# Ending every block of a 39-block kernel with the semaphore-only barrier

## The chip, the cores and the metric

One Trainium2 chip, one of its cores. The metric is the device time of one execution in microseconds (us); three runs of the kernel before give a median of 3190.18 us.

## The reference

Three transformer blocks run one after the other on an input of 512 tokens and 1024 features, all in float32. In short:

```python
x = layer_norm(a*x + 0.5*swiglu_ffn(x))                  # block 1: FFN 1024 -> 2816 -> 1024
x = layer_norm(a*x + parallel_mixers(x))                 # gated delta rule, 31-tap convolution, gates
x = layer_norm(a*x + memory_cross_attention(x, mem))     # 4 heads over 256 memory rows
x = layer_norm(a*x + 0.5*swiglu_ffn(x))
x = x + [retention(x), nsa(x)] @ w_out                   # block 2: retention beside compressed,
                                                         #   selected and window attention
x = ...neighbourhood attention and MLA, gated, then FFN  # block 3
```

Most of the arithmetic is in the products with 202 weight tiles of 128 x 2048 numbers.

## The kernel before

Activations lie feature-major in SBUF (`arena`, 56 units of 128 x 512). Each float32 weight tile is loaded by SyncE (line 185, `stream_load`), split into a high part by ScalarE (line 198, `split_hi`) and a low part by GpSimd (line 207, `stream_split_lo`), two buffers each; TensorE then makes three products a tile part (lines 228 to 230, `three_products`). The loads and splits run one or two tiles ahead of TensorE, through all the phases: the split of the first tile of a phase is made at the end of the phase before it.

The program is a row of phases, and each phase is one `nc.Block()`: a region in which every engine has its own list of instructions, and at whose end all five engines meet. There are 18 places in the source that open a block, and the program runs 39 of them: `phase_stream` (line 549) 14 times, `phase_ffn_in` (342), `phase_ffn_out` (396) and `phase_attention_pairs` (1667) three times each, `phase_head_norm` (882) and `phase_rope` (1891) twice, and one each of `phase_start` (277), the delta rule's phases (970, 1082, 1155, 1239), `phase_attention` (1482), `phase_mla_norms` (1849), `phase_norm_2` (1939), `phase_compress` (2061), `phase_retention` (2167), `phase_mla_in` (2267) and the last one in `program` (2408). The line of a block is also the line under which the profile files its barrier.

The barrier at the end of a block is not in the source; the trace shows its instructions. Every engine's sequencer issues a DRAIN. The DRAINs of TensorE, VectorE, ScalarE and SyncE each raise one counting semaphore; GpSimd's DRAIN raises none. GpSimd's sequencer then waits in an EVENT_SEMAPHORE for four arrivals, and raises a second semaphore in another EVENT_SEMAPHORE; the four others wait for that one in an EVENT_SEMAPHORE each. So GpSimd is the hub. A further barrier of this form, at line 2594, stands ahead of the first block and is made by the constructor of the program, not by a block.

GpSimd issues no DMA in this kernel: SyncE and ScalarE issue all of them. Nothing else orders work between blocks that a semaphore doesn't; apart from the splits that run ahead, the first instruction of a phase starts when the barrier lets it. A phase that ends with a layer norm (line 396, and part of those of 549) ends with ScalarE's reciprocal square root (line 490); the next phase starts with VectorE scaling by it (line 534) and ScalarE's affine step (line 526).

Of the kernel before, what the change touches and what calls it, by code (L numbers as in the profile page):

```python
# [273 lines left out]
def phase_start(K):  # L274

    nc, dram = K.nc, K.dram
    with nc.Block() as block:
        @block.sync
        def _(sp):
            sp.dma_start(K.raw[:, 0, :, :], dram["stream"][0]).then_inc(K.s("raw_loaded_0").sem, 16)  # L280
            for i in range(2):
                sp.dma_start(K.A[:, 4 * i:4 * i + 4, :], dram["x_t"][:, 4 * i:4 * i + 4, :]).then_inc(K.s(f"x_in_{i}").sem, 16)
            sp.dma_start(K.raw[:, 1, :, :], dram["stream"][1]).then_inc(K.s("raw_loaded_1").sem, 16)
            sp.dma_start(K.vecs[:, :], dram["vecs"]).then_inc(K.s("loaded").sem, 16)
            sp.dma_start(K.mats[:, :, :], dram["mats"]).then_inc(K.s("loaded").sem, 16)
            sp.dma_start(K.small[:, 0:320], dram["small"]).then_inc(K.s("loaded").sem, 16)

        @block.scalar
        def _(act):
            split_hi(K, act, 0, 1, 0, 1)  # L290
            nc.scalar.nop().then_inc(K.s("bank_free_0").sem, K.s("bank_free_0").n(2))

        @block.vector
        def _(dve):
            nc.vector.nop().then_inc(K.s("bank_free_1").sem, K.s("bank_free_1").n(2))
    K.end_block()
# [39 lines left out]
def phase_ffn_in(K, name, weight=0.5, norm=None):  # L336


    nc = K.nc
    silu, h_ready, hhi_ready = K.s("silu_ready"), K.s("h_ready"), K.s("h_hi_ready")  # L340
    sg, h = K.A[:, 52:54, :], K.A[:, 54:56, :]
    with nc.Block() as block:  # L342
        @block.sync
        def _(sp):
            stream_load(K, sp, name)
            if isinstance(norm, FirstSplit):
                sp.wait_ge(K.s("loaded").sem, 48)

        @block.gpsimd
        def _(pool):  # L350
            if norm:
                norm.pool(pool)
            stream_split_lo(K, pool, name)

        @block.tensor
        def _(pe):
            stream_pe(K, pe, name, split=norm is not None)

        @block.scalar
        def _(act):  # L360
            if norm:
                norm.act(act)

            def evac(t, g, slot, times):
                wait_bank(K, act, g, 0)
                nc.scalar.activation(sg[:, slot, :], K.ps[:, 2 * slot, :], ACT.Silu).then_inc(silu.sem, silu.n(1, times))  # L366
            stream_act(K, act, name, evac)

        @block.vector
        def _(dve):  # L370
            if norm:
                norm.dve(dve)

            def evac(t, g, slot, times):
                wait_bank(K, dve, g, 1)
                dve.wait_ge(silu.sem, silu.at(t + 1))
                nc.vector.scalar_tensor_tensor(h[:, slot, :], sg[:, slot, :], weight, K.ps[:, 2 * slot + 1, :],  # L377
                                               ALU.mult, ALU.mult).then_inc(h_ready.sem, h_ready.n(1, times))
                dve.wait_ge(h_ready.sem, h_ready.at(t + 1))
                nc.vector.nop().then_inc(K.s("bank_free_0").sem, K.s("bank_free_0").n(1, times))  # L380
                nc.vector.nop().then_inc(K.s("bank_free_1").sem, K.s("bank_free_1").n(1, times))
                at = bass.ds(t, 1) if not isinstance(t, int) else slice(t, t + 1)
                nc.vector.tensor_copy(K.hhi[:, at, :], h[:, slot:slot + 1, :]).then_inc(hhi_ready.sem, hhi_ready.n(1, times))
                dve.wait_ge(hhi_ready.sem, hhi_ready.at(t + 1))
                nc.vector.tensor_tensor(K.hlo[:, at, :], h[:, slot:slot + 1, :], K.hhi[:, at, :].bitcast(F32),
                                        ALU.subtract)
            stream_dve(K, dve, name, evac)
    K.end_block()


def phase_ffn_out(K, name):

    nc, s = K.nc, K.s
    norm = LayerNorm(K, 0, lambda eng, c: eng.wait_ge(s("sum_taken").sem, s("sum_taken").at(c + 1)),
                     K.pair[:, 8:12, :], mean_bank=0, var_bank=1)
    with nc.Block() as block:
        @block.sync
        def _(sp):
            stream_load(K, sp, name)

        @block.gpsimd
        def _(pool):
            stream_split_lo(K, pool, name)
            norm.stats_pool(pool)

        @block.scalar
        def _(act):
            stream_act(K, act, name)
            norm.stats_act(act)

        @block.tensor
        def _(pe):
            def body(t, g, uses, slot, times):
                pe.wait_ge(K.s("lo_ready").sem, g + 1)
                for j in range(2):
                    f = bass.ds(2 * t + j, 1) if not isinstance(t, int) else slice(2 * t + j, 2 * t + j + 1)
                    for m in range(KC):
                        last = three_products(K, K.ps[:, m:m + 1, :], K.whi[:, slot, 8 * j + m, :],
                                              K.wlo[:, slot, 8 * j + m, :], K.hhi[:, f, :], K.hlo[:, f, :],
                                              isinstance(t, int) and t == 0 and j == 0,  # L420
                                              isinstance(t, int) and t == TILES[name] - 1 and j == 1)
                        if isinstance(t, int) and t == TILES[name] - 1 and j == 1 and m < KC - 1:
                            last.then_inc(s("sum_ready").sem, s("sum_ready").n())
                    last.then_inc(K.s(("first_done", "tile_done")[j]).sem, 1)
            n, first = TILES[name], FIRST_TILE[name]
            body(0, first, 0, first % 2, 1)
            loops = (n - 3) // 2
            with pe.Fori(0, loops) as i:
                for j in range(2):
                    body(2 * i + (1 + j), 2 * i + (first + 1 + j), 0, (first + 1 + j) % 2, loops)  # L430
            for t in range(1 + 2 * loops, n):
                body(t, first + t, 0, (first + t) % 2, 1)
            norm.stats_pe(pe)

        @block.vector
        def _(dve):
            for m in range(KC):
                if m < KC - 1:
                    dve.wait_ge(s("sum_ready").sem, s("sum_ready").at(m + 1))
                else:  # L440
                    wait_bank(K, dve, FIRST_TILE[name] + TILES[name] - 1, 1)
                nc.vector.scalar_tensor_tensor(K.A[:, m, :], K.A[:, m, :], ALPHA, K.ps[:, m, :], ALU.mult,  # L442
                                               ALU.add).then_inc(s("sum_taken").sem, s("sum_taken").n())
            norm.stats_dve(dve)
# [98 lines left out]
def phase_stream(K, label, names, pe=None, act=None, dve=None, load=None, load_next=None, pe_last=None, presplit=None, width=T,  # L543
# [2 lines left out]

    with K.nc.Block() as block:
        @block.sync  # L550
        def _(sp):
            if load:
# [320 lines left out]
def phase_head_norm(K, label, items, scratch, eps=RMS_EPS, after=None, store=False, source=None):  # L873


    nc, s = K.nc, K.s
# [2 lines left out]

    def taken(i):  # L880
        return source[:, i, :] if source is not None else K.A[:, items[i][0], :]
    with nc.Block() as block:
        @block.scalar
        def _(act):
            def square(i):
# [75 lines left out]
def phase_gdn_matrices(K):  # L961

    nc, s = K.nc, K.s
# [3 lines left out]
        return W[:, 2 * kind + h % 2, :]  # L967
    LEVEL, DEC, EXPG, MD = range(4)
    TILES_AT = [slice(P * i, P * i + P) for i in range(NT)]
    with nc.Block() as block:  # L970
        @block.gpsimd
        def _(pool):
            for h in range(GDN_HEADS):
# [101 lines left out]
def phase_gdn_inverse(K):  # L1075

    nc, s = K.nc, K.s
# [1 line left out]
    items = [(level, h) for level in (2, 4, 8, 16, 32) for h in range(GDN_HEADS)]  # L1079
    n = len(items)  # L1080
    turns = n - GDN_HEADS
    with nc.Block() as block:
        @block.gpsimd
        def _(pool):
            for x, (level, h) in enumerate(items):
# [65 lines left out]
def phase_gdn_tokens(K):  # L1151

    nc, s = K.nc, K.s
    A, W = K.A, K.pair
    with nc.Block() as block:
        @block.tensor
        def _(pe):
            def turn(h):
# [49 lines left out]
def phase_gdn_scan(K):  # L1208
# [27 lines left out]
        return ap.rearrange("p (k s n) -> p k s n", k=2, s=2)  # L1236
    finish = [0, 2, 4, 6, 1, 3, 5, 7]
    TURNED = [0, 1, 4, 5, 6, 7]
    with nc.Block() as blk:
        @blk.vector  # L1240
        def _(dve):
            nc.vector.memset(W[:, 4:6, :], 0.0).then_inc(s("scan_zero").sem, s("scan_zero").n())
# [209 lines left out]
def phase_attention(K, label, heads, p_unit, pt_unit, load=None):  # L1452
# [26 lines left out]
    def col(at, x):  # L1479
        return K.small[:, at + x % 4:at + x % 4 + 1]  # L1480

    with nc.Block() as block:
        @block.sync
        def _(sp):
            if load:
# [141 lines left out]
def phase_attention_pairs(K, label, pairs, p_unit, pt_unit, load=None):  # L1627
# [36 lines left out]
    def cols(at, x):  # L1664
        return K.small[:, at + 2 * (x % 4):at + 2 * (x % 4) + 2]

    with nc.Block() as block:
        @block.sync
        def _(sp):
            if load:  # L1670
# [174 lines left out]
def phase_mla_norms(K):  # L1845

    nc, s = K.nc, K.s
    sq = K.pair
    with nc.Block() as block:
        @block.sync  # L1850
        def _(sp):
            sp.dma_start(sq[:, 8:13, :], K.dram["mla_w"]).then_inc(s("reloaded").sem, s("reloaded").n(16))
# [30 lines left out]
def phase_rope(K, label, chunks, matrix, cos, sin, load=None, rows=P, copies=None):  # L1883
# [4 lines left out]

    def wait_added(eng, x):
        eng.wait_ge(s("rope_added").sem, s("rope_added").at(x + 1))  # L1890
    with nc.Block() as block:  # L1891
        @block.sync
        def _(sp):
            if load:
# [41 lines left out]
def phase_norm_2(K):  # L1936

    nc, s = K.nc, K.s
    with nc.Block() as block:
        @block.vector  # L1940
        def _(dve):
            Affine(K, 0, "ln4_g", "ln4_b", split=False).dve(dve)
# [98 lines left out]
def phase_compress(K):  # L2041
# [16 lines left out]
    def hid(kind, m, g):  # L2058
        at = HID + 128 * kind + 64 * m + 32 * g
        return K.small[:, at:at + N_CMP]  # L2060
    with nc.Block() as block:
        @block.sync
        def _(sp):
            for i in range(1, 4):
# [88 lines left out]
def phase_retention(K):  # L2153
# [10 lines left out]

    def weighted(x, side):
        return W[:, 2 * (x % 3) + side, :]
    with nc.Block() as block:
        @block.tensor
        def _(pe):
            def scores(x):  # L2170
# [90 lines left out]
def phase_mla_in(K):  # L2261
# [2 lines left out]
    A, W = K.A, K.pair  # L2264
    uq = W[:, 8:11, :].rearrange("p a b -> p (a b)").rearrange("p (k n) -> p k n", k=2)
    ukv = W[:, 11:13, :].rearrange("p a b -> p (a b)")
    with nc.Block() as block:
        @block.sync
        def _(sp):
            sp.dma_start(A[:, 52:54, :], K.dram["rope_3"]).then_inc(s("reloaded").sem, s("reloaded").n(16))  # L2270
# [125 lines left out]
def program(nc, dram):  # L2396
# [8 lines left out]
    block2(K)  # L2405
    block3(K)
    last = Affine(K, 0, "ln2_g_3", "ln2_b_3", split=False)
    with nc.Block() as block:  # L2408
        @block.vector
        def _(dve):  # L2410
            last.dve(dve)
# [194 lines left out]
```

## Time and profile before

| what | value |
|---|---|
| runs, median (lowest to highest) | 3190.18 us (3188.05 to 3190.51) |
| the profiled execution | 3194.44 us, its span 3192.7 us |
| TensorE busy | 2924.4 us, 92% of the span |
| TensorE weight loads | 2282.5 us, 71%, beside the products |
| VectorE, ScalarE, GpSimd busy | 32%, 32%, 36% |
| mean granted TensorE clock | 0.95 of full speed |
| blocks (barriers) | 39, and one barrier ahead of them |

The profile is one execution on the chip. PE is TensorE, PEld its weight loads, DVE VectorE, ACT ScalarE, POOL GpSimd, SP SyncE; a q behind the name (POOLq) is the engine's sequencer, which waits, branches and issues. DRAIN and EVENT_SEMAPHORE are sequencer instructions and don't count as busy. A DRAIN is recorded from where the sequencer reaches it to where the engine's issued work is done, so a long one is mostly the engine's own last operations.

### The profile page before, as it was taken

To read this page: it belongs to the slowest core of one execution; us is meant where nothing else is said; L and a number is where in the kernel's file an instruction comes from. 1 tells how busy PE (TensorE), PEld (TensorE's weight loads), DVE (VectorE), ACT (ScalarE), POOL (GpSimd) and SP (SyncE) were. 2 spreads that over 40 slices of the span, in tenths; PEclk is the share of its full clock that TensorE was granted. 3 is DMA by queue.
4 is the path that set the end of the run, shared out by engine and by line. 5 is a ranking of instruction groups with operands and counts; after the bars stand their busy time and mean duration, and the time that the engine had idled before them with its cause. 6 is when DMAs were issued, how large, how long until landed. Compare 5 with 4: busy or idle time off the path is not lost. (4 is left out here: it accounts for less than half of the span.)

```text
span 3192.7 us, 35648 instructions
## 1 busy us (share of the span) xinstructions
PE 2924.4 (92%) x14270; PEld 2282.5 (71%) x14270; DVE 1034.9 (32%) x1727; ACT 1019.8 (32%) x1439; POOL 1162.7 (36%) x379
## 2 busy tenths in 40 slices
PE   8999999999989988889999899877899789999998
PEld 6887788886688767668878587344787436678876
DVE  2110216997334431431110300555300635431101
ACT  3331222234444223233321322244122444143312
POOL 4443443444363346144444442100344011444442
PEclk9999999999999999999999899877999889999999
DMA  4222231243100233122222124000223001122221
GB/s 153 104 92 92 79 119 66 100 144 125 67 1 28 106 119 119 40 79 92 92 95 103 42 103 160 33 3 1 83 102 125 1 24 40 66 92 92 98 87 66
DMA packets 40847, 258.01 MB, mean 81 GB/s; under 512 B 4128, under 2 KB 5536, under 8 KB 13088
## 3 DMA queue, kind: packets, MB, share of 16 engines
q1 hardware_dynamic: 37136, 248.09, 21.9%
q10 hardware_dynamic: 3600, 8.39, 0.7%
q8 instruction: 76, 1.25, 0.2%
q14 instruction: 35, 0.29, 0.0%
HBM read 243.88 MB, written 12.58 MB: 80 GB/s over the span
## 5 line engine op out<-in xcount | busy, mean ns | idle before, releaser
L207 POOL TENSOR_TENSOR weights_lo<-weights_raw,weights_hi 128x2048 fp32r<-128x2048 f32 x201 | 940.8, 4681 | 1567.5 <-ACT weights_hi L198 1567.5
L228 PE MATMUL psum<-x_hi,weights_hi 128*128 128x512 f32 (+1 forms) x2560 | 1009.3, 394 | 100.3 <-DVE x_lo L331 54.5
L229 PE MATMUL psum<-x_lo,weights_hi 128*128 128x512 f32 (+1 forms) x2560 | 1003.0, 392 | 0.0
L230 PE MATMUL psum<-x_hi,weights_lo 128*128 128x512 f32 (+1 forms) x2560 | 1002.2, 391 | 0.0
L198 ACT ACTIVATE weights_hi<-weights_raw 128x2048 fp32r<-128x2048 f32 x202 | 386.6, 1914 | 833.3 <-PE psum L230 725.8
L228 PEld LDWEIGHTS psum<-x_hi,weights_hi 128*128 128x128 f32 x2560 | 489.3, 191 | 217.8 <-issue 84.9
L230 PEld LDWEIGHTS psum<-x_hi,weights_lo 128*128 128x128 f32 x2560 | 489.1, 191 | 100.9
L229 PEld LDWEIGHTS psum<-x_lo,weights_hi 128*128 128x128 f32 x2560 | 489.8, 191 | 98.9
L377 DVE SCALAR_TENSOR_TENSOR arena<-arena,psum 128x512 f32<-128x512 f32 x66 | 45.4, 688 | 554.8 <-PE psum L230 554.8
L228 PE MATMUL psum<-h_hi,weights_hi 128*128 (+1 forms) x528 | 207.7, 393 | 7.7 <-PEq L342 7.7
L229 PE MATMUL psum<-h_lo,weights_hi 128*128 (+1 forms) x528 | 207.2, 392 | 0.0
L230 PE MATMUL psum<-h_hi,weights_lo 128*128 (+1 forms) x528 | 206.9, 392 | 0.0
L715 DVE SCALAR_TENSOR_TENSOR psum<-arena,vecs,psum 128x511 f32<-128x511 f32 (+17 forms) x240 | 159.5, 735 | 10.4 <-ACT arena L674 7.8
L442 DVE SCALAR_TENSOR_TENSOR arena<-arena,psum 128x512 f32<-128x512 f32 x24 | 16.3, 687 | 351.0 <-PE psum L230 351.0
L228 PEld LDWEIGHTS psum<-h_hi,weights_hi 128*128 128x128 f32 x528 | 100.2, 190 | 29.8 <-issue 8.8
L230 PEld LDWEIGHTS psum<-h_hi,weights_lo 128*128 128x128 f32 x528 | 100.2, 190 | 21.0
L229 PEld LDWEIGHTS psum<-h_lo,weights_hi 128*128 128x128 f32 x528 | 100.2, 190 | 20.8
L366 ACT ACTIVATE arena<-psum 128x512 f32<-128x512 f32 x66 | 39.5, 598 | 201.1 <-PE psum L230 201.1
L511 POOL TENSOR_TENSOR x_lo<-arena,x_hi 128x512 fp32r<-128x512 f32 x48 | 63.0, 1321 | 98.1 <-DVE x_hi L504 98.1
L1725 DVE TENSOR_TENSOR psum<-psum,arena 128x256 f32<-128x256 f32 (+2 forms) x64 | 36.9, 577 | 188.9 <-PE psum L1681 186.3
L1681 PE MATMUL psum<-arena 64*128 64x512 f32 (+4 forms) x256 | 92.4, 688 | 3.8 <-PEq L1891 2.7
L1911 POOL TENSOR_TENSOR pair_scratch<-arena 96x512 f32<-96x512 f32 (+1 forms) x17 | 21.4, 1265 | 187.8 <-DVEq L1918 179.7
(258 smaller groups left out, 3068.1 us busy)
## 6 DMA issues: line engine op xcount, KB each, us to landing
weights_raw<-in_stream SPq DMA_DIRECT2D x202, 1024.0 KB, 4.8
keep_gates<-arena ACTq DMA_DIRECT2D x24, 256.0 KB, 2.0
arena<-keep_gates SPq DMA_DIRECT2D x3, 2048.0 KB, 9.6
arena<-in_na_bias SPq DMA_DIRECT2D x1, 3584.0 KB, 12.9
arena<-in_x_t SPq DMA_DIRECT2D x2, 1024.0 KB, 8.0
keep_x<-arena ACTq DMA_DIRECT2D x1, 2048.0 KB, 8.5
keep_yc<-arena SPq DMA_DIRECT2D x1, 2048.0 KB, 7.0
arena<-keep_yc SPq DMA_DIRECT2D x1, 2048.0 KB, 14.0
```

The source lines that it names most:

```text
L198: K.nc.scalar.activation(K.whi[:, slot, :, :], K.raw[:, slot, :, :], ACT.Copy).then_inc(K.s("hi_ready").sem, 1)
L207: K.nc.gpsimd.tensor_tensor(K.wlo[:, 1 - slot, :, :], K.raw[:, 1 - slot, :, :], K.whi[:, 1 - slot, :, :].bitcast(F32), ALU.subtract).then_ ...
L228: K.nc.tensor.matmul(out, whi, xhi, start=start, stop=False)
L229: K.nc.tensor.matmul(out, whi, xlo, start=False, stop=False)
L230: return K.nc.tensor.matmul(out, wlo, xhi, start=False, stop=stop)
L366: nc.scalar.activation(sg[:, slot, :], K.ps[:, 2 * slot, :], ACT.Silu).then_inc(silu.sem, silu.n(1, times))
L377: nc.vector.scalar_tensor_tensor(h[:, slot, :], sg[:, slot, :], weight, K.ps[:, 2 * slot + 1, :], ALU.mult, ALU.mult).then_inc(h_ready.sem ...
L511: K.nc.gpsimd.tensor_tensor(K.xlo[:, c, :], K.A[:, first_unit + c, :], K.xhi[:, c, :].bitcast(F32), ALU.subtract).then_inc(K.s("x_split"). ...
L715: ins = nc.vector.scalar_tensor_tensor(acc[:, back:], K.A[:, 8 + c, :T - back], w, acc[:, back:], ALU.mult, ALU.add)
L1681: last = nc.tensor.matmul(K.ps[:, scores_bank(x) + side, :w], q, k[:, :w], start=True, stop=True)
L1725: nc.vector.tensor_tensor(out, out, bias, ALU.add).then_inc(s("att_bias").sem, s("att_bias").n())
L1911: nc.gpsimd.tensor_tensor(W[:rows, 12 + x % 2, :], A[:rows, c, :], cos, ALU.mult).then_inc(s("rope_cos").sem, s("rope_cos").n())
```

## The change

All 18 places open their block with an argument:

```diff
@@ phase_start @@
-    with nc.Block() as block:
+    with nc.Block(no_gpsimd_drain=True) as block:
@@ phase_stream @@
-    with K.nc.Block() as block:
+    with K.nc.Block(no_gpsimd_drain=True) as block:
@@ phase_gdn_scan @@
-    with nc.Block() as blk:
+    with nc.Block(no_gpsimd_drain=True) as blk:
```

and in the same way at the other fifteen. The description of the argument says that the engines other than GpSimd are then retired with a plain drain, and that the engines meet in a barrier made of semaphore instructions alone, with no drain on GpSimd. No other line changes.

## Rows read from the trace of the kernel before

**Rows 1.** The page, part 1: busy time, share and instructions of each engine.

```profile
PE 2924.4 (92%) x14270; PEld 2282.5 (71%) x14270; DVE 1034.9 (32%) x1727; ACT 1019.8 (32%) x1439; POOL 1162.7 (36%) x379
```

**Rows 2.** The page, part 3: every DMA queue of the core, packets, MB.

```profile
q1 hardware_dynamic: 37136, 248.09, 21.9%
q10 hardware_dynamic: 3600, 8.39, 0.7%
q8 instruction: 76, 1.25, 0.2%
q14 instruction: 35, 0.29, 0.0%
```

**Rows 3.** Line 396, 380 to 394 us: op xcount, ns min/median/max, first and last start.

```profile
L396 POOLq EVENT_SEMAPHORE  x2: 17/17/17, 392.9 to 393.0; - x2
L396 POOLq DRAIN  x1: 1356/1356/1356, 381.0 to 381.0; - x1
...
L396 PEldq DRAIN  x1: 3000/3000/3000, 389.2 to 389.2; - x1
L396 ACTq DRAIN  x1: 679/679/679, 392.2 to 392.2; - x1
L396 SPq EVENT_SEMAPHORE  x1: 17/17/17, 393.0 to 393.0; - x1
...
L396 DVEq EVENT_SEMAPHORE  x1: 21/21/21, 393.0 to 393.0; - x1
L396 PEldq EVENT_SEMAPHORE  x1: 51/51/51, 393.0 to 393.0; - x1
```

**Rows 4.** Timeline, 391 to 394.7 us: start, us, engine, line, idle before.

```profile
392.19 0.66 ACT L490 ACTIVATE psum<-psum,vecs 128x512 f32<-128x512 f32 x1 [1.74 <-PE psum L479]
393.14 1.88 DVE L534 TENSOR_TENSOR arena<-arena,psum 128x512 f32<-128x512 f32 x3 [4.66 <-PEq L396]
...
393.87 1.52 ACT L526 ACTIVATE arena<-arena,vecs 128x512 f32<-128x512 f32 x2 [1.02 <-DVE arena L534]
```

**Rows 5.** Line 549 over the whole span: the barriers of all 14 streaming blocks.

```profile
L549 POOLq EVENT_SEMAPHORE  x28: 17/17/17, 497.6 to 2796.9; - x28
...
L549 POOLq DRAIN  x14: 1351/4708/7249, 480.5 to 2784.9; - x14
L549 ACTq DRAIN  x14: 259/679/1931, 488.9 to 2796.1; - x14
```

**Rows 6.** Line 549, 1232 to 1239 us: one barrier.

```profile
L549 POOLq DRAIN  x1: 4711/4711/4711, 1233.2 to 1233.2; - x1
...
L549 ACTq DRAIN  x1: 414/414/414, 1237.5 to 1237.5; - x1
```

**Rows 7.** Timeline, 1236.5 to 1242 us, around that barrier.

```profile
1233.22 4.61 POOL L207 TENSOR_TENSOR weights_lo<-weights_raw,weights_hi 128x2048 fp32r<-128x2048 f32 x1 [1.81 <-ACT weights_hi L198]
...
1237.51 0.38 ACT L1823 ACTIVATE arena<-psum 128x256 f32<-128x256 f32 x1 [2.49 <-PE psum L1444]
...
1238.20 1.88 DVE L534 TENSOR_TENSOR arena<-arena,psum 128x512 f32<-128x512 f32 x3 [50.57 <-PEq L549]
```

**Rows 8.** Line 1667, 2075 to 2237 us: the barrier of an attention block.

```profile
L1667 POOLq DRAIN  x1: 34/34/34, 2075.1 to 2075.1; - x1
...
L1667 DVEq DRAIN  x1: 730/730/730, 2235.2 to 2235.2; - x1
```

**Rows 9.** Line 2408, the last block's barrier.

```profile
L2408 POOLq DRAIN  x1: 41/41/41, 3183.7 to 3183.7; - x1
...
L2408 SPq DRAIN  x1: 7/7/7, 3192.4 to 3192.4; - x1
```

**Rows 10.** Who waited for whom, whole span: us in total, times, longest.

```profile
DVE arena L534 <- PEq L396: 14.0, 3, 4.7
...
POOL weights_lo L308 <- POOLq L277: 7.5, 1, 7.5
```

More of the change, by code:

```diff
@@ L341, in phase_ffn_in @@
     sg, h = K.A[:, 52:54, :], K.A[:, 54:56, :]
-    with nc.Block() as block:
+    with nc.Block(no_gpsimd_drain=True) as block:
         @block.sync
@@ L395, in phase_ffn_out @@
                      K.pair[:, 8:12, :], mean_bank=0, var_bank=1)
-    with nc.Block() as block:
+    with nc.Block(no_gpsimd_drain=True) as block:
         @block.sync
@@ L881, in taken @@
         return source[:, i, :] if source is not None else K.A[:, items[i][0], :]
-    with nc.Block() as block:
+    with nc.Block(no_gpsimd_drain=True) as block:
         @block.scalar
@@ L969, in phase_gdn_matrices @@
     TILES_AT = [slice(P * i, P * i + P) for i in range(NT)]
-    with nc.Block() as block:
+    with nc.Block(no_gpsimd_drain=True) as block:
         @block.gpsimd
@@ L1081, in phase_gdn_inverse @@
     turns = n - GDN_HEADS
-    with nc.Block() as block:
+    with nc.Block(no_gpsimd_drain=True) as block:
         @block.gpsimd
@@ L1154, in phase_gdn_tokens @@
     A, W = K.A, K.pair
-    with nc.Block() as block:
+    with nc.Block(no_gpsimd_drain=True) as block:
         @block.tensor
@@ L1480, in col @@
         return K.small[:, at + x % 4:at + x % 4 + 1]
-    with nc.Block() as block:
+    with nc.Block(no_gpsimd_drain=True) as block:
         @block.sync
@@ L1665, in cols @@
         return K.small[:, at + 2 * (x % 4):at + 2 * (x % 4) + 2]
-    with nc.Block() as block:
+    with nc.Block(no_gpsimd_drain=True) as block:
         @block.sync
@@ L1848, in phase_mla_norms @@
     sq = K.pair
-    with nc.Block() as block:
+    with nc.Block(no_gpsimd_drain=True) as block:
         @block.sync
@@ L1890, in wait_added @@
         eng.wait_ge(s("rope_added").sem, s("rope_added").at(x + 1))
-    with nc.Block() as block:
+    with nc.Block(no_gpsimd_drain=True) as block:
         @block.sync
@@ L1938, in phase_norm_2 @@
     nc, s = K.nc, K.s
-    with nc.Block() as block:
+    with nc.Block(no_gpsimd_drain=True) as block:
         @block.vector
@@ L2060, in hid @@
         return K.small[:, at:at + N_CMP]
-    with nc.Block() as block:
+    with nc.Block(no_gpsimd_drain=True) as block:
         @block.sync
@@ L2166, in weighted @@
         return W[:, 2 * (x % 3) + side, :]
-    with nc.Block() as block:
+    with nc.Block(no_gpsimd_drain=True) as block:
         @block.tensor
@@ L2266, in phase_mla_in @@
     ukv = W[:, 11:13, :].rearrange("p a b -> p (a b)")
-    with nc.Block() as block:
+    with nc.Block(no_gpsimd_drain=True) as block:
         @block.sync
@@ L2407, in program @@
     last = Affine(K, 0, "ln2_g_3", "ln2_b_3", split=False)
-    with nc.Block() as block:
+    with nc.Block(no_gpsimd_drain=True) as block:
         @block.vector
```

## The prediction

> **What bounds the kernel now.** I read the busy times first. TensorE is busy for 92% of the span [rows 1], and the three other compute engines for about a third each, so most of the time is products that no barrier touches; a change to the barriers can only act in the seams between the 39 blocks. The chain that ended last reaches back only through the last 9 us of the span and says nothing of the other seams, so I went on to the barrier's own instructions, block by block, under the line of each block. Rows 3 are one such barrier, the one that ends the first FFN's output phase. The reader is to see three things there. Each engine has a DRAIN that starts where its sequencer runs out of instructions and lasts until its issued work is done. The sequencer of GpSimd reaches its DRAIN at 381.0 us and has done with it at 382.4 us (1356 ns). The last to arrive is ScalarE, whose DRAIN starts at 392.2 and lasts 679 ns, to 392.9. So GpSimd stands ready 10.5 us before the barrier can open, and its DRAIN is not what anybody waits for. Then come two semaphore instructions of GpSimd, at 392.9 and 393.0, and one of each other engine.
>
> What the whole barrier costs is seen beside it [rows 4]: ScalarE's last operation ends at 392.19 + 0.66 = 392.85 us, VectorE's first of the next phase starts at 393.14. The seam is 0.29 us, and everything that a different barrier could win or lose is a change to these 0.29 us, times 39.
>
> **What is removed.** GpSimd's DRAIN, 39 times. It could be dear in two ways, and both are read off.
>
> First, it could have DMAs to wait for. The queue table has two queues of the hardware's dynamic kind and two of instructions, and none that GpSimd feeds [rows 2]; where GpSimd has nothing of its own in flight its DRAIN takes 34 to 41 ns [rows 8, 9]. The long ones, 1351 to 7249 ns in the 14 streaming blocks [rows 5], are GpSimd's own last subtraction or addition: in rows 6 and 7 the DRAIN of 4711 ns starts with the split of 4.61 us and ends with it.
>
> Second, GpSimd could be the last to arrive. I went through the 39 barriers in this way and compared where each DRAIN ends. ScalarE, VectorE, TensorE or SyncE is last in all of them. The closest is the one at 1238 us [rows 6]: GpSimd's DRAIN ends at 1233.2 + 4.7 = 1237.9, ScalarE's at 1237.5 + 0.4 = 1237.9, a tie. Its seam [rows 7] goes from 1237.51 + 0.38 = 1237.89 to 1238.20, 0.31 us, so the tie costs at most 0.02 us over the 0.29 of rows 4. The typical one has GpSimd ahead by 5 to 12 us, and the widest by 160 us (rows 8: 2075.1 against 2235.2 + 0.7). So what hides the removed DRAIN is the tail of the other engines, the layer norm of rows 3 or the last evacuations, and the removal is worth 39 times nothing, with 0.02 us at the tie. The stall that would be dropped isn't one; next late is who was late before.
>
> One wait in the list of waits looks like GpSimd's barrier and isn't: POOLq L277 is charged with 7.5 us [rows 10]. That is the first block, where everybody waits for the first weight tile; the charge goes to the releasing engine, as the 14.0 us on PEq L396 do, and neither falls with a DRAIN.
>
> **What is added.** The four other engines keep a DRAIN, but a plain one. In the kernel before their arrival is an update that the DRAIN itself makes, as there is no arrival instruction of theirs in rows 3: one EVENT_SEMAPHORE each, which is the wait for the release. With a plain DRAIN and a barrier of semaphore instructions alone, the arrival must be an instruction of its own behind the DRAIN, one more on each of four queues. Only that of the engine that arrives last lies on the path. Nothing is queued behind it on that engine but the release wait, and for that one everyone waits, so its price is paid in full in each seam; after the barrier the first instruction of the next phase starts later by the same amount, and nothing hides that, since the next phase has no instruction before it.
>
> Its price has bounds in the rows. From below it is the duration alone: 17 ns on ScalarE or SyncE, 21 on VectorE, 51 on TensorE [rows 3]. From above it is the pitch of GpSimd's two consecutive semaphore instructions, 392.9 to 393.0, 0.1 us. Between them lies the mean step of the seam: 0.29 us hold four handoffs (last operation to GpSimd's wait, wait to raise, raise to the release waits, these to the next operation), 0.07 us each. I take 0.08 us, since a step of that mean size with rounding is nearest and this step also carries its own 17 to 21 ns. Bounds: 39 x 0.017 = 0.7 us and 39 x 0.1 = 3.9 us; sum: 39 x 0.08 = 3.1 us. The hub's two instructions and the four release waits I cost at nothing, as they are there before.
>
> **The sum.** The profiled execution took 3194.44 us (span 3192.7 us) and would take 3194.44 + 3.1 = 3197.5 us. The median of the runs lies 4.3 us below the profiled execution, so the forecast for the median is 3190.18 + 3.1 = 3193.3 us, +0.1%. A measurement of this kernel can tell about 0.2% (6.4 us) from no change, so this counts as no change.
>
> **The rivals.**
>
> *A longer relay (slower).* The argument's barrier need not have one hub. If the engines hand the arrival along in a row and the release back, five engines make eight hops instead of the four handoffs of today. At the 0.07 us of a handoff that is 0.56 instead of 0.29 us; the seam grows by 0.27, times 39 is 10.5 us: 3200.7 us, slower. It decides for slower from 0.165 us more for each seam (6.4 / 39). For it speaks that a semaphore-only form is said to be another barrier than the one with drains; against it, that the hub scheme in rows 3 is already made of EVENT_SEMAPHORE instructions once the DRAINs are over, and could be kept. The Trainium skill, page Runtime: NRT & Kernel Launch, section on the preamble and postamble, describes such a serpentine over five engines for the runtime's own barrier, at 355 ns (44 ns a hop, eight hops). No row here has that form; against the 0.29 us of the seam in rows 4 it would add some 0.07 us by that figure, an estimate from that page, 2.5 us in all, and the case would fall inside no change.
>
> *The arrival costs nothing.* The arrival may still be made by the plain DRAIN, or the extra instruction may overlap the DRAIN's end. Then nothing on the path changes and the time is 3190.2 us. This is also the case in which the change does nothing but drop 39 hidden DRAINs. For it speaks rows 3, where the sequencers of four engines stand at their DRAIN long before it ends.
>
> *A direct exchange (a little faster).* If all engines raise and wait for one count, GpSimd's two instructions leave the path and one arrival comes in: four handoffs become three, -0.07 x 39 = -2.7 us, 3187.5 us. Even a barrier that cost nothing would give only 39 x 0.29 = 11.3 us, so faster by 6.4 us needs more than half of the seam to go.
>
> *GpSimd runs past the barrier.* Without its DRAIN GpSimd's last subtraction may go on into the next block. Nobody gains, as shown, but the port or the next wait could be met otherwise; in the seam of rows 7 that is under 0.1 us once, and I give it no time.
>
> **How the numbers follow.** The separate arrival 0.50 (3193.3, by its bounds 3190.9 to 3194.1); arrival at no cost 0.22 (3190.2); relay 0.17 (3200.7); direct exchange 0.08 (3187.5); something not seen 0.03, half of it faster. The runs before differ by 2.5 us, which goes on both ends. The range must leave out at most 0.2: it takes in the direct exchange down to 3186.0 and above reaches to 3200.0, so that the lower part of the relay (a seam longer by 0.08 to 0.25 us) is in it and its upper part out. Faster by over 0.2% (below 3183.8) has 0.02; slower by over 0.2% (above 3196.6) has the relay with most of its 0.17 and a share of the unseen, 0.16; the rest, 0.82, is within 0.2%.
>
> **What would show each step right or wrong.** In the profile after, no DRAIN of GpSimd under a block's line (one stays at 2594, ahead of the blocks); two EVENT_SEMAPHORE instead of one for each other engine in each of 39 barriers, so some 156 instructions more and 39 fewer; the seam of rows 4 at 0.37 instead of 0.29 us, and ScalarE still last there. The relay would show in EVENT_SEMAPHORE starts that follow one another over the engines and a seam of 0.5 us or more. A direct exchange would show GpSimd with the same pair as everybody. The prediction would be wrong if GpSimd's DRAIN did something that its record doesn't show, if seams changed by more than 0.165 us, or if time moved away from the seams, say in TensorE's products [rows 1], where the change has no business.

## The result and the profile after

| | runs | median, us | lowest to highest |
|---|---|---|---|
| before | 6 | 3188.98 | 3185.42 to 3190.51 |
| changed | 6 | 3198.72 | 3192.68 to 3203.67 |

The ratio is 1.0026, interval 1.0014 to 1.0038: slower by 8.3 us of the kernel before, 4.5 to 12.1. (The two medians of the table lie 9.7 us apart; the text goes by the ratio on record.) The forecast was 3193.3 us with a range of 3186.0 to 3200.0. Measured again in two later sessions, the ratio was 1.0012 (0.9999 to 1.0025) and 1.0015 (1.0006 to 1.0024), where the forecast stood at 1.0010. So the changed kernel is slower by 0.1 to 0.3%, about what one measurement can tell from nothing; over all runs together it is 4.9 us with an error of 0.9.

The profiled execution of the changed kernel took 3192.68 us, less than that of the kernel before (3194.44). Its page:

```profile
span 3190.9 us, 35765 instructions
...
PE 2918.2 (91%) x14270; PEld 2279.8 (71%) x14270; DVE 1029.6 (32%) x1727; ACT 1019.5 (32%) x1439; POOL 1163.1 (36%) x379
```

TensorE's busy time is 6.2 us lower than in rows 1, with the same number of instructions. A single execution of either kernel can come out ahead: the mean granted clock of this one was 0.957, that of the kernel before 0.954, and how time goes with this clock is read further down.

The barrier that answers to rows 3, in the changed kernel (line 396, 377 to 394 us; engine, instruction, count, ns min/median/max, first and last start):

```profile
L396 DVEq EVENT_SEMAPHORE  x2: 21/21/21, 385.8 to 390.3; - x2
L396 PEldq EVENT_SEMAPHORE  x2: 51/51/51, 389.4 to 390.3; - x2
L396 ACTq EVENT_SEMAPHORE  x2: 17/17/17, 390.1 to 390.3; - x2
L396 POOLq EVENT_SEMAPHORE  x2: 17/17/17, 390.1 to 390.2; - x2
L396 DVEq DRAIN  x1: 4897/4897/4897, 380.8 to 380.8; - x1
L396 PEldq DRAIN  x1: 3002/3002/3002, 386.4 to 386.4; - x1
L396 ACTq DRAIN  x1: 679/679/679, 389.4 to 389.4; - x1
L396 SPq EVENT_SEMAPHORE  x1: 17/17/17, 390.3 to 390.3; - x1
```

There is no DRAIN of GpSimd any more. ScalarE, VectorE and TensorE have two EVENT_SEMAPHORE each where rows 3 had one: the first is the arrival, a separate instruction behind the DRAIN (ScalarE: DRAIN 389.4 + 0.679, arrival at 390.1), the second the wait for the release. SyncE's first lies outside this window. GpSimd has its two, as before, and is still the hub. ScalarE still arrives last. In the whole program there are 117 instructions more, 156 arrivals less 39 DRAINs (35765 against 35648).

The seam that answers to rows 4, in the timeline (start, duration, engine, line):

```profile
389.37 0.66 ACT L490 ACTIVATE psum<-psum,vecs 128x512 f32<-128x512 f32 x1 [1.74 <-PE psum L479]
390.38 1.28 DVE L534 TENSOR_TENSOR arena<-arena,psum 128x512 f32<-128x512 f32 x2 [4.72 <-PEq L396]
```

From the end of ScalarE's operation, 389.37 + 0.66 = 390.03 us, to the start of VectorE's it is 0.35 us, against 0.29.

And the one that answers to rows 7, where GpSimd and ScalarE were level:

```profile
1229.62 4.61 POOL L207 TENSOR_TENSOR weights_lo<-weights_raw,weights_hi 128x2048 fp32r<-128x2048 f32 x1 [1.81 <-ACT weights_hi L198]
...
1233.92 0.38 ACT L1823 ACTIVATE arena<-psum 128x256 f32<-128x256 f32 x1 [2.49 <-PE psum L1444]
...
1234.67 0.69 DVE L534 TENSOR_TENSOR arena<-arena,psum 128x512 f32<-128x512 f32 x1 [52.20 <-PEq L549]
```

From 1233.92 + 0.38 = 1234.30 to 1234.67 it is 0.37 us, against 0.31. GpSimd's split ends at 1234.23 and isn't waited for; nothing came of that, since ScalarE ends at 1234.30.

Compared seam by seam, from the end of the last DRAIN to the first operation behind the barrier, the 38 seams between blocks are longer by 0.049 to 0.112 us, the median by 0.062. The trace gives three sizes: mostly 0.053 us where ScalarE arrives last (0.049 to 0.060), about 0.07 where VectorE does (0.060 to 0.077), and 0.112 at the one seam where TensorE does. The sum is 2.5 us.

### The profile page after: what moved, and what is told of

Read it like the earlier page. It is cut to its first block and busy times, and to the rows that moved or that the text cites. A ratio compares the mean times of both kernels' runs of the same rounds, so it can differ in the third digit from the quotient of the medians.

```text
span 3190.9 us, 35765 instructions
## 1 busy us (share of the span) xinstructions
PE 2918.2 (91%) x14270; PEld 2279.8 (71%) x14270; DVE 1029.6 (32%) x1727; ACT 1019.5 (32%) x1439; POOL 1163.1 (36%) x379
## 6 DMA issues: line engine op xcount, KB each, us to landing
arena<-in_na_bias SPq DMA_DIRECT2D x1, 3584.0 KB, 12.9
arena<-keep_yc SPq DMA_DIRECT2D x1, 2048.0 KB, 13.8
```

## The experiments

**The kernel before against itself, and how far a ratio can be trusted.** No line is changed.

> The kernel before, unchanged, against itself. Every theory: ratio 1.000. It tells how far two medians of one program lie apart on this chip, which is what the other ratios of this call are to be read against. If it comes out at 1.001 or more either way, half or more of the measured 1.0026 of the change can be spread of the runs.

Measured: 0.9989 (0.9979 to 0.9998), with 12 runs against 35. In a later session:

> The kernel before against itself, again: 1.000, clock 0.956. Its distance from 1 is the error of such a ratio.

Measured: 0.9995 (0.9986 to 1.0004). A third run of the same program came about unmeant. The kernel before was to have bare nops in its seams:

```diff
@@ Kernel.end_block @@
             s.base += s.pending
             s.pending = 0
+        nc = self.nc
+        for _ in range(8):
+            for eng in (nc.sync, nc.tensor, nc.vector, nc.scalar, nc.gpsimd):
+                eng.nop()
```

> The kernel before, with eight sequencer nops on each engine behind each of the 38 blocks but the last. A nop of a sequencer takes about what an arrival instruction takes, so each seam grows by eight times that, 0.4 to 0.7 us, 15 to 27 us in all, if time of a seam is paid once: ratio 1.005 to 1.0085. Theory of amplification (a seam's delay moves TensorE's half-speed stretches and costs three times what the seam shows): 45 us or more, 1.014.

Measured: 0.9995 (0.9985 to 1.0005). The trace has 35648 instructions, as many as the kernel before: a nop that neither waits nor raises is not in the program that ran, so it says nothing of seams and is one more control. The seams of its trace sum to 10.2 us, against 10.1 in the kernel before, so the expected 15 to 27 us failed with the edit. The three miss 1 by 0.0011, 0.0005 and 0.0005, all downwards, and the interval of the first (up to 0.9998) leaves out 1, though the program is the same: the intervals are somewhat too narrow. The first also meets the condition of its expectation (0.001 or more either way), so a large part of the 1.0026 of the first measurement can be spread of the runs, and it needed repeating. A ratio of 1.0008, what the seams alone would give, can't be told from 1.

**The changed kernel again.**

> The changed kernel again. Arrival theory (each seam is longer by one semaphore instruction, some 0.05 to 0.12 us, 39 times, about 2.5 us, and nothing else): ratio 1.0008, and the ratio of 1.0026 falls back. Theory of a cost outside the seams (a further 6 us): 1.0026 again, and the blocks themselves longer in the trace.

Measured: 1.0012 (0.9999 to 1.0025).

> The changed kernel a third time. Its seams are longer by 2.5 us in all in its traces. If that is all that it costs beside the spread of half-speed stretches: ratio 1.0008 plus or minus 0.0012, and mean granted clock somewhere in the range of the control's. If the change also lowers the clock for good, as in the two measurements so far (0.954 against 0.956): 1.002 and clock 0.954 again.

Measured: 1.0015 (1.0006 to 1.0024), mean granted clock of its runs 0.9543, beside 0.9557 for the kernel before in the same session and 0.9554 for its control (in the earlier session 0.9541 beside 0.9559 and 0.9569). The seams of its profiled execution are longer by 2.4 us in all. The ratio lies between the two expected, within the 0.0012 allowed to the seams alone; the clock is the lower one.

**The DRAIN put back.** The arrival stays separate and only GpSimd's DRAIN returns, as its last instruction in each block.

```diff
+@contextlib.contextmanager
+def block_with(nc):
+    with nc.Block(no_gpsimd_drain=True) as block:
+        yield block
+
+        @block.gpsimd
+        def _(pool):
+            pool.drain()
...
-    with nc.Block(no_gpsimd_drain=True) as block:
+    with block_with(nc) as block:
```

> The changed kernel, with a DRAIN put back as the last instruction of GpSimd in each of the 39 blocks, so that only the separate arrival of the other four is left of the change. Arrival theory: as the changed kernel, seams longer by 0.05 to 0.12 us, ratio 1.0008. Theory that the missing DRAIN costs the further 6 us (GpSimd running on into the next block): the 6 us come back, and the ratio is below that of the changed kernel in this call by 0.002.

Measured: 1.0022 (1.0009 to 1.0034); 1.0012 for the changed kernel in the same session.

> The changed kernel with GpSimd's DRAIN put back, again. Its seams are as long as those of the changed kernel (2.4 against 2.5 us in all). If the DRAIN is worth nothing: equal to the changed kernel of this call within 0.0012. If the 3 us that it was slower last time are the DRAIN's: 0.001 above the changed kernel again.

Measured: 1.0019 (1.0007 to 1.0030), beside 1.0015. Its GpSimd DRAINs, all 39 under one line (columns as in rows 3):

```profile
L109 POOLq DRAIN  x39: 34/1357/7254, 0.7 to 3190.0; - x39
```

They are as short and as long as in rows 5 and 8, and the seam of the first FFN is that of the changed kernel, 389.95 + 0.66 = 390.61 to 390.96, 0.35 us:

```profile
389.95 0.66 ACT L503 ACTIVATE psum<-psum,vecs 128x512 f32<-128x512 f32 x1 [1.74 <-PE psum L492]
390.96 1.28 DVE L547 TENSOR_TENSOR arena<-arena,psum 128x512 f32<-128x512 f32 x2 [4.72 <-PEq L104]
```

So the DRAIN can be there or not; the seam's length comes from the arrivals alone. The theory that GpSimd running on costs the further 6 us falls: it asked for a ratio 0.002 below that of the changed kernel, and with the DRAIN back nothing is won. Whether the DRAIN itself costs something can't be told: the two ratios are higher by 0.0010 and 0.0004, inside their intervals, and its seams sum to 2.4 us like the others.

**The same delay by another instruction.** The kernel before with its own barriers; behind each of 38 blocks every engine raises a counting semaphore of its own once, or four times.

```diff
@@ Kernel.end_block @@
             s.pending = 0
+        for eng, name in ((self.nc.sync, "sp"), (self.nc.tensor, "pe"), (self.nc.vector, "dve"), (self.nc.scalar, "act"),
+                          (self.nc.gpsimd, "pool")):
+            for _ in range(1):        # 4 in the second kernel
+                eng.nop().then_inc(self.s("count_" + name).sem, 1)
```

> The kernel before, with its own barriers, and behind each of 38 blocks one nop that raises a counting semaphore on each of the five engines. That is the same kind of delay as the separate arrival (some 0.07 us in a seam, 2.7 us in all) by another instruction in another place. Seams alone: ratio 1.0008 against the kernel before, mean granted clock as before (0.956). Theory that a longer seam also costs TensorE clock: clock 0.954 as in the changed kernel, and 1.002 as there. Theory that the changed kernel's lower clock has to do with its barrier's form: clock 0.956 here.

> The same with four of them on each engine in each of 38 seams, about 0.28 us a seam, 10.6 us in all. Seams alone: ratio 1.0033. If each us of seam costs three through the clock: 30 us, 1.010. If the extra of the changed kernel is a chance of where its half-speed stretches fall, not a thing that grows with the seams: 1.0033 plus or minus 0.001, whatever the clock.

Measured: 1.0018 (1.0009 to 1.0027) with one, 1.0044 (1.0030 to 1.0059) with four. The seam behind the first FFN with one:

```profile
392.06 0.66 ACT L494 ACTIVATE psum<-psum,vecs 128x512 f32<-128x512 f32 x1 [1.74 <-PE psum L483]
393.11 1.88 DVE L538 TENSOR_TENSOR arena<-arena,psum 128x512 f32<-128x512 f32 x3 [4.75 <-PEq L400]
```

392.72 to 393.11, 0.39 us, 0.10 more than in rows 4. With four:

```profile
393.08 0.66 ACT L494 ACTIVATE psum<-psum,vecs 128x512 f32<-128x512 f32 x1 [1.74 <-PE psum L483]
394.41 1.88 DVE L538 TENSOR_TENSOR arena<-arena,psum 128x512 f32<-128x512 f32 x3 [5.03 <-PEq L400]
```

393.74 to 394.41, 0.67 us, 0.38 more. Over the 38 seams the traces sum to 3.8 and 13.8 us. Measured are 5.7 us (2.9 to 8.6) and 14 us (10 to 19). The second seam is longer than the 0.28 us expected, and its ratio lies just above the 1.0033 plus 0.001. The clock of the first came out at 0.9546, that of the second at 0.9553, beside 0.9549 (standard error 0.0004) for the kernel before in the same session: neither is clearly lower.

**A whole barrier more.** `self.nc.all_engine_barrier()` in the same place of the kernel before.

> The kernel before with a second all-engine barrier, with drains, behind each of 38 blocks. It measures a whole barrier with nothing to wait for: the seam of 0.27 to 0.29 us less the first instruction's issue, some 0.2 us, 38 times: 7.6 to 11 us, ratio 1.0024 to 1.0034. Amplification by three would be 1.008 or more.

Measured: 1.0044 (1.0029 to 1.0058), 14 us (9 to 19), with a clock of 0.9535 (0.0006); more than the 7.6 to 11 us expected. The seam:

```profile
390.15 0.66 ACT L491 ACTIVATE psum<-psum,vecs 128x512 f32<-128x512 f32 x1 [1.74 <-PE psum L480]
391.44 1.28 DVE L535 TENSOR_TENSOR arena<-arena,psum 128x512 f32<-128x512 f32 x2 [5.00 <-PEq L149]
```

390.81 to 391.44, 0.63 us, 0.34 more than in rows 4; times 38 that is 12.9 us, and over all 38 seams the trace sums to 14.5 us more. The added DRAINs of GpSimd, which has nothing to do there:

```profile
L149 POOLq DRAIN  x38: 34/41/108, 7.7 to 3195.5; - x38
```

From the two larger ones: a us of seam costs about a us, 14 measured against 13.8 and 14 against 14.5 in the traces, whether by one instruction or by a barrier. The amplification by three (each us of seam costing three through the clock) is excluded, as it would be 1.008 to 1.010 for these two. The smaller delays cost about 2 us more than their seams (5.7 against 3.8 here, 4.9 against 2.5 in the changed kernel over all its runs), the larger ones don't; that is inside the error for the one raise, and no run here explains it.

**Where the DRAIN does matter.** GpSimd gets DMAs of its own: at the end of each block four copies of 1 MB from HBM to HBM, which nobody needs, in the kernel before and in the changed one. From the second block on it first waits for those of the block before.

```diff
+        @block.gpsimd
+        def _(pool):
+            if LATE["blocks"]:
+                pool.wait_ge(K.late, 16 * 4 * LATE["blocks"])
+            for j in range(4):
+                pool.dma_start(K.dram["spare"][j], K.dram["stream"][j]).then_inc(K.late, 16)
+            LATE["blocks"] += 1
```

> The kernel before, with work for GpSimd's DMA queue added: at the end of each of the 39 blocks GpSimd issues four copies of 1 MB from HBM to HBM that nobody in the block needs. If its DRAIN waits for DMAs that it has issued, GpSimd becomes the last to arrive and each block ends when its copies have landed: DRAIN records of 10 us and more, and hundreds of us more in all. If the DRAIN has nothing to do with DMAs, it stays at 0.04 to 5 us.

> The same copies in the changed kernel. With no DRAIN on GpSimd the barrier opens while they are in flight, so the blocks are as long as without them, but for the DMA engines' share and for a wait of GpSimd at the end of the next block. The difference between the two kernels is then what the argument saves where GpSimd does issue DMAs, some 10 us a block; if the DRAIN has nothing to do with DMAs, the two are equal within 0.3%.

Measured: 3434.56 us with the default barriers, 1.077 (1.073 to 1.080); 3245.96 us with the changed ones, 1.018 (1.014 to 1.022); two runs each. A queue appears that rows 2 do not have (first kernel, page part 3):

```profile
q0 software_dynamic: 4992, 163.59, 13.6%
```

GpSimd's DRAINs in the first:

```profile
L107 POOLq DRAIN  x39: 13507/14987/20961, 2.5 to 3416.8; - x39
```

In the second there are none:

```profile
L107 POOLq EVENT_SEMAPHORE  x78: 17/17/17, 7.7 to 3240.2; - x78
L107 PEldq DRAIN  x39: 8/3002/5953, 0.8 to 3217.6; - x39
```

So GpSimd's DRAIN does wait for the DMAs that GpSimd has issued, 13.5 to 21 us here: in the trace each of the 39 ends after the last copy has landed, 37 of them 0.52 to 0.58 us after it, the two others 1.15 and 1.22. It makes GpSimd the last to arrive at 28 of the 39 barriers, by 222 us in all; at the other eleven it lies beside the work of others, by up to 143 us. So no more than 222 us could be saved, 5.7 a block and not the 10 expected; measured are 188.6 us, 4.8 a block, and the kernel without the DRAINs is still 57.5 us above the kernel before. TensorE's busy time doesn't bear on it, 2927.8 us with the DRAINs and 2926.8 without.

## Where the rest of the time is: TensorE's clock

The seams of the changed kernel explain 2.5 us. All its 29 runs have a mean of 3196.7 us (standard error 0.8), the 115 runs of the kernel before, controls included, 3191.8 (0.3): 4.9 us (0.9). Taken by session the means lie 10.0, 4.1 and 5.0 us apart. (Not among the 115 are the six runs of the first measurement, which have no clock on record, and the three beside the copies.) Each run lists its mean granted clock. Among the 115 runs of the kernel before alone, a clock lower by 0.001 goes with 1.8 us more. The means are 0.9541 (0.0003) for the changed kernel and 0.9558 (0.0001) for the other, which by that slope goes with 3.0 us. 2.5 and 3.0 make 5.5 us, near the 4.9. This is a relation between runs and doesn't show what moved the clock. The kernel with the DRAIN put back has 0.9544 and 3198.5 us (1.1), 1.7 us over the changed one, with an error of about 1.4.

The traces don't show those 3 us in TensorE's products. Its busy time was 2918.2, 2923.2 and 2920.9 us in the three profiled executions of the changed kernel and 2924.4, 2921.3, 2916.0 and 2922.0 in the four of the kernel before: 2920.8 and 2920.9 in the mean. Their spans are 5.0 us apart in the mean (3194.5 and 3189.5), all of it idle time of TensorE: 2.4 us in the seams and 2.7 inside the blocks. These three executions had clocks of 0.957, 0.955 and 0.956, above the mean of their kernel, so they need not show what the others lost. In the two with the DRAIN put back (clock 0.954) TensorE was busy for 2927.9 and 2926.7 us, 6.4 us more than in the kernel before, and idle inside the blocks for 1.2 us more. What lengthens the blocks is thus not the same in all traces.

The clock has two levels, 2.4 and 1.2 GHz, and in the records it falls to the lower one for some stretches, 273 to 297 us in all in each of nine traces. Whole blocks differ by where these lie. The stretch of the second FFN's output phase and that of block 2's attention, line 1667, before (stretch, length, busy of PE, PEld, DVE, ACT, POOL, granted clock, DMA share, GB/s):

```profile
1645.20:1778.10 132.90, 130.53 (x552) 103.48 (x552) 10.31 (x16) 27.84 (x21) 55.76 (x15) 1.00 0.25 87
...
2075.00:2236.00 161.00, 115.66 (x768) 69.42 (x768) 90.92 (x292) 72.21 (x241) 0.00 (x0) 0.77 0.01 2
```

and after:

```profile
1640.10:1774.70 134.60, 132.12 (x552) 104.65 (x552) 10.32 (x16) 27.84 (x21) 55.72 (x15) 0.99 0.24 86
...
2072.50:2234.40 161.90, 116.99 (x768) 69.72 (x768) 90.94 (x292) 72.23 (x241) 0.00 (x0) 0.76 0.01 2
```

In the first, with 552 products in both, PE is busy for 132.12 instead of 130.53 us and the clock is 0.99 instead of 1.00. One short half-speed stretch near the phase's start, behind the seam in which TensorE stood still, makes the phase 1.7 us longer. It is there in five of five traces of the longer barrier (the changed kernel's three, the DRAIN put back, two) and in one of four of the kernel before. But this phase is picked: in the same phase of the first and third FFN such a stretch stands in four of eight cases of the kernel before and in five of ten of the longer barrier. The attention phase shows the range. A control:

```profile
2077.20:2238.80 161.60, 116.48 (x768) 70.04 (x768) 90.94 (x292) 72.13 (x241) 0.00 (x0) 0.76 0.01 2
```

another control:

```profile
2078.00:2236.60 158.60, 113.44 (x768) 68.13 (x768) 90.93 (x292) 72.11 (x241) 0.00 (x0) 0.78 0.01 2
```

the changed kernel in its second session:

```profile
2081.30:2245.10 163.80, 120.00 (x768) 71.56 (x768) 90.92 (x292) 72.33 (x241) 0.00 (x0) 0.73 0.01 2
```

the kernel with four raises in each seam:

```profile
2093.70:2250.70 157.00, 111.80 (x768) 67.30 (x768) 91.08 (x292) 72.11 (x241) 0.00 (x0) 0.78 0.01 2
```

and the one with a whole barrier more, whose seams are as long as those with four raises:

```profile
2083.90:2247.70 163.80, 119.95 (x768) 71.45 (x768) 90.97 (x292) 72.39 (x241) 0.00 (x0) 0.73 0.01 2
```

VectorE is busy for 90.9 to 91.2 us in all twelve traces; TensorE for 110.8 to 120.0, with the clock between 0.78 and 0.73, and the phase follows it, 157.0 to 163.8 us. With the shorter delay the phase is long in all six traces (160.8 to 163.8; the kernel with one raise 161.8), with none it is 158.0 to 161.6 in four, and with the two longest delays it is the shortest of all (157.0) and as long as the longest (163.8). So what the clock does in a phase shifts with when the work of that phase starts, and not steadily in the direction of the delay. That the mean clock is lower with the new barrier is seen in both later sessions, with and without GpSimd's DRAIN; by which path is not settled. The one raise a seam, which has nothing of that form, has 0.9546 (0.0004), but the kernel before had 0.9549 (0.0004) in that session, so it tells neither for a delay of any kind nor for the barrier's form.

## Why the prediction was right, and what in it was off

*GpSimd's DRAIN is never waited for*: right within 0.1 us. In the trace that the prediction read it was last in none of the 39 barriers, at the tie by 0.03 us; in two of the three other traces of the same program it is last at one barrier, the one before the tie, by 0.065 and 0.013 us. Put back into the changed kernel it leaves the seams as they are. That it would matter with DMAs of GpSimd's own, and that rows 2 show none, was the reason given, and the pair of kernels with copies shows it.

*The arrival becomes an instruction of its own*: right, to the instruction (117 more), with GpSimd still the hub. The relay and the direct exchange are out: the order of the semaphore instructions is that of rows 3. The Trainium skill's page Runtime: NRT & Kernel Launch, in its breakdown of the preamble and postamble, describes its serpentine for the runtime's own barrier. The 0.35 us of the seam here come near its 355 ns by chance: the trace has GpSimd as the hub and no relay.

*Its price, 0.08 us*: mis-sized upward. Measured are 0.053 us with ScalarE last and about 0.07 with VectorE last, 2.5 us in all instead of 3.1. The mean step of 0.07 from rows 4 would have been nearer; the rounding up toward the pitch of GpSimd's pair was not needed. The raises behind the barrier, at 0.10 us each, show that the price of such an instruction depends on where it stands. Why it is lower behind a DRAIN was not tried.

*The whole*: 3193.3 us, +3.1, against +4.9 us over all runs (+8.3 in the first measurement). Beside the size of the arrival, what the prediction had wrong is its last sentence, that the change has no business outside the seams: it put that term at nothing. Over all runs some 2.4 us, with an error of 0.9, lie outside them. They come with a lower mean clock in the runs; in the traces they stand as idle time of TensorE inside the blocks in one set and as longer products in the other, and their cause stays open. The range held that, by its share of a rival that turned out to be wrong: the right width for another reason. The first median, 3198.72 us, lies in what the prediction called slower by over 0.2% (above 3196.6) and the mean of all 29 runs at its edge; the chance of 0.16 for it was tied to the relay and left such a term out. In the later sessions the ratio was 1.0012 and 1.0015, well inside 0.2%.

No version beats the kernel before: of the barrier forms tried its own is the cheapest, as its arrival comes with the DRAIN.

## What to carry to other kernels

Before taking a wait out, read who arrives last at it: a DRAIN that ends well ahead of the barrier (here mostly by 2 to 160 us) is free, and the form that leaves it out may have a longer path for the others. Leave GpSimd's DRAIN out where GpSimd issues DMAs of its own that need not land before the block ends; that is the only case here in which it paid. For effects of 0.1% put controls of the unchanged kernel beside the change, and read each run's clock with its time.

## What was not expected of the hardware

GpSimd's DRAIN behind four 1 MB copies took 15.0 us at the median and ended 0.5 us after the last copy had landed; it outlasted the other engines by 222 us in all, in a kernel that the copies made 246 us slower. A whole all-engine barrier with nothing to wait for costs 0.34 us in a seam (14.5 us over 38), one more semaphore instruction behind a DRAIN 0.053 to 0.112 us by engine. And the new barrier, with delays of 0.05 to 0.1 us at the phases' starts, comes with a mean granted clock lower by 0.001 to 0.002, at 1.8 us for each 0.001, while two delays of much the same size, 0.38 and 0.34 us, gave the shortest attention phase and one of the two longest.
